# Three of the 192 expert weight loads cut into nine transfers each

## The reference, cut to what matters

```python
for e in range(N_EXPERTS):                       # 8 experts
    he = jax.nn.silu(t @ w1[e]) * (t @ w3[e])    # w1, w3: 1024 x 3584
    out = out + gates[:, e:e + 1] * (he @ w2[e]) # w2: 3584 x 1024
```

## Time and profile before

| | us |
|---|---|
| median of 3 runs | 1228.58 (1227.88 to 1232.32) |
| profiled execution, first to last instruction | 1225.3 |
| median less that span (what lies around it) | 3.3 |

### The profile page before, as it was taken

The page is one execution under the profiler, slowest core; times in us unless marked ns, Lnnn a source line. Parts: engine busy times, 40 slices in busy tenths (PEclk is TensorE's granted clock), DMA queues, the critical chain, the costliest instruction groups (busy, mean ns, idle before and its releaser), DMA issues.

```text
span 1225.3 us, 27750 instructions
## 1 busy us (share of the span) xinstructions
PE 1150.1 (94%) x12548; PEld 687.8 (56%) x12549; DVE 325.8 (27%) x546; ACT 262.1 (21%) x402; POOL 90.9 (7%) x134
## 2 busy tenths in 40 slices
PE   8999999999999999999999978899997889999785
PEld 8888888888986546446345423434642343464232
DVE  6977776667875000000001000000100000010000
ACT  6885344345751100000000000000000000000000
POOL 5302200000001000101000100100010010001001
PEclk9999999999999999999999999999999999999998
DMA  7559565652179999999999999999999999999993
GB/s 259 192 172 326 189 198 182 195 183 101 61 282 424 426 420 361 391 426 425 421 423 424 416 421 426 424 422 424 426 412 425 426 421 422 424 425 414 427 423 104
DMA packets 75304, 421.58 MB, mean 344 GB/s; under 512 B 6130, under 2 KB 42607, under 8 KB 50608
## 3 DMA queue, kind: packets, MB, share of 16 engines
q1 hardware_dynamic: 70000, 413.16, 83.4%
q0 software_dynamic: 5184, 6.61, 2.2%
HBM read 417.45 MB, written 4.72 MB: 345 GB/s over the span
## 4 chain that ended last, share of the span: by engine, by line
PE 74%; DMA 21%; DVE 2%; ACT 1%; issue 1%; POOL 0%; POOLq 0%; SPq 0%; DVEq 0%; ACTq 0%
PE ps L1289 30%; DMA w_ring<-in_moe_w_dram 21%; PE ps L1312 15%; PE ps L1027 7%; PE ps L744 5%; PE ps L746 5%; PE ps L745 5%; PE ps L1032 3%; PE ps L1302 1%; PE ps L1274 0%; PE ps L865 0%; PE ps L1258 0%; POOL head_rstd L622 0%; PE ps L783 0%; PE ps L946 0%
## 5 line engine op out<-in xcount | busy, mean ns | idle before, releaser
L1289 PE MATMUL ps<-w_ring,expert_in 128*32 128x512 f32 (+1 forms) x5120 | 490.9, 540 | 37.1 <-DMA w_ring<-in_moe_w_dram 37.1
L1289 PEld LDWEIGHTS ps<-w_ring,expert_in 128*32 128x32 f32 x5120 | 177.4, 110 | 342.4 <-issue 275.8
L1312 PE MATMUL ps<-w_ring,expert_hT 128*32 128x256 f32 x4480 | 251.8, 383 | 17.3 <-DMA w_ring<-in_moe_w_dram 17.3
L1312 PEld LDWEIGHTS ps<-w_ring,expert_hT 128*32 128x32 f32 x4480 | 145.3, 111 | 118.7 <-DMA w_ring<-in_moe_w_dram 26.8
L1796 DVE TENSOR_TENSOR w_lo<-w_raw,w_hi 128x2048 fp32r<-128x2048 f32 (+2 forms) x63 | 127.5, 2050 | 34.6 <-ACT w_hi L1373 34.5
L1027 PE MATMUL ps<-act_both,w_hi 128*128 128x512 f32 x352 | 122.4, 396 | 0.0
L1373 ACT ACTIVATE w_hi<-w_raw 128x2048 fp32r<-128x2048 f32 (+2 forms) x62 | 104.2, 1716 | 2.9 <-DMA w_raw<-in_mla_w_kvb_dram 2.9
L2357 DVE TENSOR_TENSOR expert_h<-expert_h,ps 128x896 f32<-128x896 f32 x20 | 21.8, 1088 | 294.1 <-PE ps L1289 294.0
L1032 PE MATMUL ps<-act_both,w_lo 128*128 128x256 f32 x352 | 91.3, 280 | 0.0
L1759 ACT ACTIVATE expert_hT<-ps 128x896 f32<-128x896 f32 x20 | 17.7, 916 | 279.2 <-PE ps L1302 279.2
L705 POOL DMA_INDIRECT out_dram<-expert_out,slot_row x20 | 31.4, 1569 | 588.5 <-ACT expert_out L1775 584.8
(11 more groups left out here) (360 smaller groups left out, 993.3 us busy)
## 6 DMA issues: line engine op xcount, KB each, us to landing
w_ring<-in_moe_w_dram SPq DMA_DIRECT2D x192, 1792.0 KB, 40.4
w_raw<-in_ffn_w_dram SPq DMA_DIRECT2D x33, 1024.0 KB, 5.3
w_raw<-in_lru_w_in_dram SPq DMA_DIRECT2D x8, 1024.0 KB, 5.5
w_raw<-in_mla_w_o_dram SPq DMA_DIRECT2D x4, 1024.0 KB, 5.1
w_raw<-in_lru_w_out_dram SPq DMA_DIRECT2D x4, 1024.0 KB, 4.9
w_raw<-in_mla_w_in_dram SPq DMA_DIRECT2D x8, 352.0 KB, 7.0
w_raw<-in_mla_w_qb_dram SPq DMA_DIRECT2D x4, 576.0 KB, 3.9
w_raw<-in_mla_w_kvb_dram SPq DMA_DIRECT2D x2, 1024.0 KB, 12.7
```

The lines of the kernel that those rows point to most:

```text
L1289: ins = pe.matmul(ps[j * STRIP:(j + 1) * STRIP, 2 * g + b, 0:wide], in_x[:, c, k, g * STRIP:(g + 1) * STRIP], w[:, j * PART + at:j * PART ...
L1312: return pe.matmul(ps[j * STRIP:(j + 1) * STRIP, bank, at:at + DOWN_COLS], hT[:, a:a + STRIP], w, start=first and at == 0, stop=last and ( ...
```

## The change

The unit u = 8 (the first w3 unit) of the experts n = 2, 4 and 6, that is g = 56, 104 and 152, is no longer loaded by one DMA of 128 partitions. It is loaded by nine: one of partitions 0 to 63, then eight of 8 partitions each, for 64 to 71, 72 to 79 and so on to 127. The bytes, the buffer, the source and the waits ahead are the same. All nine raise the same semaphore by 16, so `landing` now counts transfers (`ring_transfers`) where it counted loads (`ring_loads`).

```diff
+    SPLIT_UNITS = [n * N_BODY + M_W3 for n in (2, 4, 6)]
+    LOW = P // 2
+    LOW_ROWS = 8
+
+    def transfers(g):
+        return 1 + (P - LOW) // LOW_ROWS if g in SPLIT_UNITS else 1
+
+    def ring_transfers(i, n):
+        return sum(transfers(g) for g in range(i, n, RING))
...
             if isinstance(n, int):
                 g = n * N_BODY + u
-                return g % RING, 16 * (g // RING + 1)
+                return g % RING, 16 * ring_transfers(g % RING, g + 1)
             i = u % RING
-            return i, 16 * (ring_loads(i, E * N_BODY) + u // RING + 1)
+            return i, 16 * (ring_transfers(i, E * N_BODY) + u // RING + 1)
...
-                    sp.dma_start(ring_raw[slot][:].rearrange("p (o n) -> p o n", o=1), src).then_inc(ring_landed[slot], 16)
+                    dst = ring_raw[slot][:].rearrange("p (o n) -> p o n", o=1)
+                    if static and n * N_BODY + u in SPLIT_UNITS:
+                        sp.dma_start(dst[0:LOW], src[0:LOW]).then_inc(ring_landed[slot], 16)
+                        for p in range(LOW, P, LOW_ROWS):
+                            sp.dma_start(dst[p:p + LOW_ROWS], src[p:p + LOW_ROWS]).then_inc(ring_landed[slot], 16)
+                    else:
+                        sp.dma_start(dst, src).then_inc(ring_landed[slot], 16)
```

## The result

| | before | after |
|---|---|---|
| median | 1229.23 us (1227.88 to 1232.32, 4 runs) | 1274.51 us (1270.22 to 1279.48, 4 runs) |
| ratio, 95% interval | | 1.0369 (1.0348 to 1.0390) |
| span of the profiled execution | 1225.3 us | 1277.7 us |

The kernel is 45.3 us slower. The forecast was +16 us and its range ended at +35.

What follows compares the result with a forecast made beforehand. The prediction took the loads to bound the kernel; 1225.3 + 0 (issue) + 16 (shared ways) gave 1241.3 us of span, with 3.3 us around it 1244.6 us, 1.3% slower; the range ran from 1221 to 1264 us.

Steps and rivals of the forecast that it cites:

- Bounds and the unit of the sum: Whole kernel: the loads set the end; one row of 14,336 bytes takes a DMA engine 0.536 us.
- (1) Issue: SP at each split unit: 24 more issues in all at 0.33 us, 2.7 us a unit, hidden by the queue; cost 0.
- (2) Who carries the rows: Split units: the same eight engines carry every eight-row transfer, 12 rows more over three units, the others 12 fewer; 6.4 us each way.
- (3) The loaded half is the early one: End of the loads: the engines given more rows are those that finish early, so the end moves by -6.4 us.
- plateau of 0.50: DMA share near the loads' end before the change: read as eight engines through at about 1196 us, eight still working.
- rival A: Split units and end: ways into SBUF have room to spare, so clean rebalancing gives 1222.2 us; chance 0.25.
- rival B: End of the loads: free ways, but the engines given more rows are the late ones, 1235.0 us; chance 0.05.
- The fetches' share: Instruction fetches, 0.5% of 16 engines' span: 98 us of engine time, 12 us each if eight engines bear it.
- (4) Who else writes there: Split units: engines sharing ways into sets of eight partitions slow down, +10 to +45 us, taken as +16; chance 0.60.
- +45: Upper bound for three split units: eight engines bunch at the same few ways at once, in us.
- +12.8 us: Low bound for three split units: fair, well spread sharing of the ways, net +4.3 us a unit.
- (5) PE: PE after each split unit: late landings cause some idling, narrow experts let it catch up; not the bound at +16 us.

Runs made afterwards that it cites:

- e11: The changed kernel, but only unit 1 of expert 0 is split, into the same nine transfers, with no other load under way; 1229.47 us against 1228.93 before.
- e7: The changed kernel, but the split units load only partitions 0 to 63, by eight eight-partition DMAs with rows four apart; 1227.04 us against 1228.01 before.
- e2: The changed kernel, but the eight partitions of each small transfer lie four apart; 1276.97 us, ratio 1.0386 to before.
- e12: The changed kernel, but only unit 1 of expert 0 is split, with each small transfer's partitions four apart; 1227.04 us against 1228.93 before.
- e1: The changed kernel, but the three units are loaded by two DMAs of 64 partitions each; 1265.02 us against 1228.94 before.
- e3: The changed kernel, but the three units are loaded by eight DMAs of 16 neighbouring partitions each; 1258.60 us, ratio 1.0242 to before.
- e8: The changed kernel, but only the unit of expert 6 is split; 1245.29 us against 1228.01 before.
- e4: The changed kernel, but only the unit of expert 2 is split; 1239.41 us, ratio 1.0076 to before.
- e9: The changed kernel, but the three units load only partitions 0 to 63, by one DMA of 64 partitions; 1244.63 us against 1228.01 before.
- e10: The changed kernel mirrored: eight eight-partition DMAs, rows four apart, load partitions 0 to 63, then one DMA loads 64 to 127; 1259.95 us against 1228.93 before.

## Why the prediction was wrong, step by step

**Bounds and the unit of the sum: right.** The loads set the end, and the change in the loads' end is the change in the time.

**(1) Issue: right in effect, wrong in size.** The eight-row issues took 0.89 us in the median, not 0.33, and the nine of unit 56 took from 571.21 to 578.88:

```profile
571.21 0.59 SPq L570 DMA_DIRECT2D w_ring<-in_moe_w_dram  x1
572.01 6.66 SPq L572 DMA_DIRECT2D w_ring<-in_moe_w_dram  x8
578.88 57.48 SPq L574 DMA_DIRECT2D w_ring<-in_moe_w_dram  x12
```

That is 7.7 us for the nine, where nine at 0.33 us would take 3.0. The queue of some 27 us hid it: the DMA share stays at 0.95 and above in the slow windows.

**(2) Who carries the rows: right.** Alone in flight, the eight-row transfers keep the share at 0.51, half of the engines (e11). The Trainium skill's rule ("DMA: Bandwidth & Descriptors", why a DMA increments its semaphore by 16 and not by 1) agrees with that number; which engines they are no row shows.

**(3) The loaded half is the early one: wrong.** I took the plateau of 0.50 for one clean half. e7 shows that two of the late engines are among the loaded. This term is +6.4 us and not -6.4, so by this reading rival A could not have come about even with free ways; it would have been rival B's 1235. The fetches' share had told me that an uneven load exists, not where it sits.

**(4) Who else writes there: the term that failed.** The direction was right, the size was +16 where 41 us of rate loss were found (and the bounds were +13 and +45). Two things were wrong in it. The +12.8 us counted the loss only for engines that share a way; in the stream the whole core runs at about half rate, every row at 0.89 us or more in the change's first stretch, for 20 to some 30 us around a unit of 4.3 us. And what I put the +45 down to, bunching at neighbouring partitions, makes no difference in the stream (e2), though it does where the unit is alone (e11 against e12). The Trainium skill's page "SBUF — State Buffer" (Door 1) is borne out for a transfer that runs alone: two 64-partition transfers go at 207 GB/s for each unit of share, half of 424, and by its ports e12's rows are one to a port and run at 416. The prediction's four row times for an eight-row transfer alone came out as 2.7 (424/155). That the rest of a saturated stream slows down with them this section does not say.

**(5) PE: right.** Idle PE appears once at unit 56 (9.05 us) and PE does not become the bound. At unit 104 it comes in four gaps (1.18, 4.96, 2.10 and 6.04 us) and not in one.

**Chances and range.** The forecast's case held 0.60 and came true in its direction, with a price near its worst bound, though not for the reason of that bound. I cut the range at +35 though the bound was +45. With no row for the price, the upper end belonged in the range.

**What stays open.** Why everybody slows down. It fits that writes to a contested way block writes behind them on a path that the engines share, but no run isolates this; e11 only says that all rows are slow, and that more is lost than sharing explains. One rival stands untested: every edit moves the rows read from HBM together with the partitions written, so no run separates engines that collide at the source from engines that collide on the way into SBUF. Loading the same source rows into other partitions would. A small foreign write into a spare buffer beside whole units would tell; it was not tried, since no buffer of that size lies free. Also open is why the rate loss grows from unit to unit where both halves of a unit hold foreign rows (7.6, 12.5, 15.9 us in e1; 8.7, 10.2, 11.5 in e3; e8 against e4), and doesn't where only one half does, the low one in e9 and the upper one in e10. Which engines serve the instruction fetches was inferred from the tail, not seen.

No version faster than before came out of it. To relieve the late engines, rows of their partitions would have to be carried by others, and that is just what costs.

## What to carry to other kernels

When a load stream is saturated as here, don't divide a tile's load by partitions: the transfers cost little, but the whole stream drops to half rate for far longer than the tile takes, as far as these runs tell because engines leave their own partitions. If a load must be cut, cut it by columns over all 128 partitions; eight such pieces in each of three units cost 2 us or nothing where eight by partitions cost 30. Read GB/s and DMA share together: 0.95 to 1.04 with 152 to 247 GB/s is contention, a low share is engines without work. And before shifting work from late engines to early ones, establish which engines are late; a plateau at 0.50 gives their number, not their names.

## What the runs showed of the hardware that I had not expected

- One split unit of 1792 KB halves the rate of all loads for 20 to some 30 us (e8: 206 to 247 GB/s between 1025 and 1050) at a DMA share near 1, and all sixteen engines are slowed: no row between 604 and 618 of the change took under 0.89 us, against 0.535 at full rate.
- Eight engines that write single rows four partitions apart run at full speed when alone (133 GB/s at a share of 0.32), rows next to each other at little over a third of that speed (79 at 0.51).
- About two engines of sixteen can set the end of a 350 MB stream: in e7 the share stands at 0.15 and 0.11 for the last 10 us and the time is unchanged.
